# Gate matrices from two fp32r products, weighed twice by ACT, with a ring of three groups of one-hots

## The reference, cut to what matters

```python
q = (xb @ w_q).reshape(P_BLOCK, P_HEADS, 2, P_DKEY // 2)
s = einsum('thcd,hckd->thck', q, keys)
s_top, i_top = lax.top_k(s, 16)
cand = s_top[:, :, 0, :, None] + s_top[:, :, 1, None, :]
cand_idx = i_top[:, :, 0, :, None] * 128 + i_top[:, :, 1, None, :]
best, pos = lax.top_k(cand.reshape(..., 256), 16)
experts = take_along_axis(cand_idx.reshape(..., 256), pos)
gate = softmax(best)                       # 8 heads x 16 experts per token
act = gelu(einsum('thkd,td->thk', u_tab[experts], xb))
out = einsum('thk,thkd->td', gate * act, v_tab[experts])
```

## Time and profile before

| what | value |
|---|---|
| time, median of 3 runs | 5639.94 us (5639.61 to 5642.14) |
| the profiled execution's own time | 5643.49 us |
| its span, first to last instruction | 5641.7 us |
| mean granted PE clock | 0.907 of full speed |
| PE matmul busy | 4789.9 us (85%) |
| DVE busy | 2920.5 us (52%) |
| ACT busy | 1496.9 us (27%) |
| POOL busy | 1332.2 us (24%) |
| gate matmuls, L1912 | 2048 records, 249.9 us busy |
| weighing, L1812 | 1024 instructions, 312.5 us busy |
| one-hots, L1644 | 256 instructions, 381.8 us busy |

### The profile page before, as it was taken

How to read it: one execution, slowest core, us unless ns; L and a number is a source line. 1 busy time by engine, 2 the same in 40 slices (tenths; PEclk the granted TensorE clock), 3 DMA queues, 4 the chain that set the end, 5 groups by cost and what they waited for, 6 DMA issues and landing times. The chain is left out here.

```text
span 5641.7 us, 58879 instructions
## 1 busy us (share of the span) xinstructions
PE 4789.9 (85%) x22999; PEld 3849.3 (68%) x22999; DVE 2920.5 (52%) x4345; ACT 1496.9 (27%) x2767; POOL 1332.2 (24%) x571
## 2 busy tenths in 40 slices
PE   7885536667899999899998896666799999899998
PEld 2664316656688887788886364655688887788886
DVE  0124455431498884266664103751588883366665
ACT  1000100000145565222222001310255474222222
POOL 0000000000144444344443000000144443344442
PEclk9995558878999999999999897778999999999999
DMA  5210100002356686555554422002466686555552
GB/s 196 75 38 0 37 15 1 1 31 82 102 161 170 178 227 189 168 190 190 197 197 151 171 70 60 1 34 82 120 163 163 172 241 180 173 190 199 194 189 95
DMA packets 491349, 718.29 MB, mean 127 GB/s; under 512 B 46745, under 2 KB 341266, under 8 KB 468530
## 3 DMA queue, kind: packets, MB, share of 16 engines
q1 hardware_dynamic: 486466, 697.76, 39.5%
q0 software_dynamic: 4608, 16.78, 0.9%
HBM read 556.81 MB, written 153.40 MB: 126 GB/s over the span
## 5 line engine op out<-in xcount | busy, mean ns | idle before, releaser
L1880 PE MATMUL ps<-h_parts,u_parts 128*128 128x512 f32 x6144 | 1432.0, 393 | 62.5 <-POOL u_parts L1847 53.2
L2104 PE MATMUL ps<-w_parts,v_parts 128*128 128x512 f32 x6144 | 1397.5, 390 | 36.4 <-DVE w_parts L2089 36.4
L1880 PEld LDWEIGHTS ps<-h_parts,u_parts 128*128 128x128 f32 x6144 | 1152.0, 189 | 300.6 <-POOL u_parts L1847 53.8
L2104 PEld LDWEIGHTS ps<-w_parts,v_parts 128*128 128x128 f32 x6144 | 1156.2, 188 | 277.7 <-POOL v_parts L2075 37.2
L1847 POOL TENSOR_TENSOR u_parts<-u_turned,u_parts 128x1024 fp32r<-128x1024 f32 x256 | 658.2, 2571 | 2281.6 <-ACT u_parts L1800 2281.4
L2089 DVE TENSOR_TENSOR w_parts<-w_rows,w_parts 128x512 fp32r<-128x512 f32 x256 | 625.7, 2444 | 480.3 <-ACT w_parts L2068 480.3
L2075 POOL TENSOR_TENSOR v_parts<-v_rows,v_parts 128x1024 fp32r<-128x1024 f32 x256 | 615.2, 2403 | 817.8 <-ACT v_parts L2066 817.8
L194 PE MATMUL ps<-h,arena 128*128 128x264 f32 (+2 forms) x2176 | 488.7, 388 | 97.8 <-DMA arena<-in_even_w_out_dram 33.9
L194 PEld LDWEIGHTS ps<-h,arena 128*128 128x128 f32 (+1 forms) x2176 | 413.4, 190 | 174.4 <-DMA arena<-in_even_w_out_dram 34.3
L2066 ACT CAST v_parts<-v_rows 128x1024 fp32r<-128x1024 f32 x256 | 268.9, 1050 | 988.5 <-PE ps L2104 962.7
L1793 DVE STREAM_TRANSPOSE u_turned<-u_rows 128x1024 f32<-128x1024 f32 x256 | 317.1, 1239 | 301.3 <-POOL u_parts L1847 261.5
(11 more groups left out here) (457 smaller groups left out, 3920.3 us busy)
## 6 DMA issues: line engine op xcount, KB each, us to landing
u_rows<-in_peer_u_dram SPq DMA_DIRECT2D x1024, 128.0 KB, 3.6
v_rows<-in_peer_v_dram SPq DMA_DIRECT2D x128, 1024.0 KB, 4.9
hidden_tiles<-hidden SPq DMA_DIRECT2D x256, 256.0 KB, 3.5
gate_matrices<-h SPq DMA_DIRECT2D x64, 1024.0 KB, 7.2
gates<-gate_matrices SPq DMA_DIRECT2D x32, 2048.0 KB, 7.9
hidden_in<-hidden_tiles SPq DMA_DIRECT2D x256, 256.0 KB, 3.8
arena<-in_ada_w_dram SPq DMA_DIRECT2D x24, 2048.0 KB, 8.0
w_ring<-in_peer_w_q_dram SPq DMA_DIRECT2D x8, 2048.0 KB, 11.3
```

The lines of the kernel that those rows point to most:

```text
L1880: ins = mm(ps[:, n % 2, :], q.uTs[:, n % 3, wp, k, :], q.hs[:, xp, k, :], start=k == 0 and (wp, xp) == (0, 0), stop=k == DT - 1 and wp == 1)
L2104: ins = nc.tensor.matmul(ps[:, o, :], q.vs[:, n % 3, vp, o * P:(o + 1) * P], q.ws[:, n % 3, wp], start=n == 0 and (vp, wp) == (0, 0), stop ...
```

## The change

The shares are split into two fp32r numbers at each `settle`, a high part and the rest, held in `s.rs2`, a buffer that otherwise only the head norms of the mixers use. The one-hots buffer gets four parts per quad instead of two (row one-hot, column one-hot, row one-hot times the rest, row one-hot times the high part), in fp32r, and three slots instead of six, so its size stays. ACT makes both products. PE multiplies both with the column one-hot, as two fp32r matmuls that add up in PSUM.

```diff
-GATE_RING = 6
+GATE_RING = 3
...
             dve.wait_ge(q.chosen.sem, q.chosen.at(t + 1))
+            now_t = slice(t * P, (t + 1) * P)
+            link(v.tensor_copy(q.share[:, 0, now_t], q.choice[:, 2, now_t]))
+            link(v.tensor_tensor(q.share[:, 1, now_t], q.choice[:, 2, now_t], f32(q.share[:, 0, now_t]), ALU.subtract))
...
-                v.tensor_tensor(q.hot[:, k % GATE_RING], s.iota[:].unsqueeze(1).unsqueeze(1).to_broadcast(eight),
+                hot = q.hot[:, k % GATE_RING]
+                v.tensor_tensor(hot[:, 0:2], s.iota[:].unsqueeze(1).unsqueeze(1).to_broadcast(eight),
...
         for i in range(4):
-            row = q.hot[:, k % GATE_RING, 0, i, :]
-            ins = nc.scalar.mul(row, row, q.choice[:, 2, 4 * k + i:4 * k + i + 1])
+            hot, at = q.hot[:, k % GATE_RING, :, i, :], slice(4 * k + i, 4 * k + i + 1)
+            nc.scalar.mul(hot[:, 2], f32(hot[:, 0]), f32(q.share[:, 1, at]))
+            ins = nc.scalar.mul(hot[:, 3], f32(hot[:, 0]), f32(q.share[:, 0, at]))
...
                         for i in range(4):
-                            ins = mm(ps[:, 2 + k % 4, i * P:(i + 1) * P], q.hot[:, k % GATE_RING, 0, i, :],
-                                     q.hot[:, k % GATE_RING, 1, i, :], start=True, stop=True)
+                            for part in (3, 2):
+                                ins = mm(ps[:, 2 + k % 4, i * P:(i + 1) * P], q.hot[:, k % GATE_RING, part, i, :],
+                                         q.hot[:, k % GATE_RING, 1, i, :], start=part == 3, stop=part == 2)
...
-            q.hot = whole("onehots", [P, GATE_RING, 2, 4, P])
+            q.hot = s.sb(f"onehots{layer}", [P, GATE_RING, 4, 4, P], second, F32R)
+            q.share = s.rs2[:, :, 0:T].bitcast(F32R)
```

## The result

The changed kernel takes 5944.0 us (median of 4 runs, 5937.1 to 5953.5), the one before 5641.0 beside it: ratio 1.0533 [1.0511, 1.0554], 303 us slower. The forecast was 5815 in a range of 5750 to 5900. The direction was right, the size was not: 303 us in place of 175.

A forecast was written before the change was run, and what follows sets the result against it. PE bounds the kernel before, ACT the gate stretches after. A 27.7, B 27.7, C 30 and the rest 2 make 87.4 us a layer, 175 in all: 5818 on the profiled execution, 5815 as median, range 5750 to 5900.

The forecast's parts named there:

- A: First stretch making gate matrices in layer 0 (1660 to 1746 us): 17.3 us from slower units plus 10.4 store waits, 27.7.
- B: Second stretch making gate matrices in layer 0 (1820 to 1906 us): the same growth as A, 27.7 us.
- C: Third stretch making gate matrices in layer 0 (1985 to 2217 us), 64 quads in 26 units: growth of 30 us.
- ACT becomes the bound, 9.87 us a unit: Three-quad units: twelve more multiplications at 0.293 us raise ACT from 6.36 to 9.87 us, above PE's 8.14.
- The fp32r record at 0.109 us: PE's gate products: a 128-column fp32r record taken like the f32 one, 0.108 us, 0.87 us a quad, no gain or loss.
- the rival of slow fp32r records: Gate products on PE: fp32r records at 0.233 us add 253 us in place of the main case, 5893; chance 0.22.
- So the ring adds no wait of its own beyond the first unit: One-hots in a ring of three: gates and one-hots are ready before ACT wants them, so no term for the ring.
- The lead: Ring of three: it takes away the lead with which ACT could have started; no price of its own.
- Store waits, exposed and 5.2 us each: ACT's gate copies waiting for gate stores, hidden under PE before: two each in A and B, 10.4 us per stretch.
- The rival that they shrink: Gate-store waits: slower units give stores more room, 48 us less, 5767; chance 0.12.
- the 0.9 that I had named as a sign against me: PE's granted clock in A and B: a value under 0.9 would show the prediction wrong.
- The clock rival: An idler PE drops to the 1.2 GHz level: 6200 in some 60 units, 5940 for a third of it; chance 0.06.

The follow-up runs named there:

- doubling alone: Kernel before, ring of six and f32 products kept, with four more ACT multiplications (by ones) per quad: 5833.4 us, ratio 1.0324.
- ring alone: Kernel before with only the ring of one-hots cut from six to three quads: 5768.4 us, ratio 1.0228.
- e5: Kernel before with a single fp32r product per token (rest of the share left out), ring of six: 5602.1 us, ratio 0.9926.
- e10: Kernel before with a ring of three, and SP issuing older gate stores ahead of the hidden stores: 5713.5 us, ratio 1.0130.
- e11: Changed kernel with six unused 512-column matmuls (the filler) on PE in A and B units of three or more quads: 5943.7 us, ratio 1.0523.

## Why the prediction was wrong, step by step

Growth of the three stretches in us (first gates to start of the last), forecast against runs:

| stretch | forecast | doubling alone | ring alone | the change |
|---|---|---|---|---|
| A | 27.7 | 27.3 | 17.4 | 42.0 |
| B | 27.7 | 27.7 | 17.6 | 44.6 |
| C | 30 | 28.4 | 24.4 | 54.8 |

- **ACT becomes the bound, 9.87 us a unit: right.** Multiplications stand 0.29 us apart, also with fp32r outputs, and undisturbed units take 9.6 to 9.9. The Trainium skill (ScalarE: Activation LUTs, What ACT_TABLE_LOAD costs) gives an ACTIVATE with one pointer operand 280 ns + 0.833 ns a column, of which some 93 ns overlap with the next. The estimate from it for 128 columns is 294 ns apart, and the trace agrees with 0.293 us. The forecast's terms for A, B and C hit the doubling alone within 2 us each. In A that is partly luck: up to the last hidden product it takes 104.1 us there, forecast 104.5, but 3.0 less before the second hidden product, 4.5 more in the two store waits, and 1.8 less in the others.
- **The fp32r record at 0.109 us: right.** 24 of them take 2.63 us (1660.75 to 1663.38 in the rows above), 12 take 1.29 in e5. So the rival of slow fp32r records is out. The Trainium skill (TensorE: Matmul & The Clock Gate, Back-to-back issue gap) has about 81 ns each for a stream of 128-column products. Here the trace does not agree: neither form goes under 0.108 us.
- **"So the ring adds no wait of its own beyond the first unit": wrong, and this is the step that failed.** The ring costs 127 us alone. I followed undisturbed units of three quads, where it holds (9.9 us), and laid the quads of each unit side by side. I put this term at nothing. But a ring of three is closed over DVE, ACT and PE: the one-hot of quad k waits for the gates of k-3, these for a PSUM bank, that for ACT's copy of k-7, and ACT copies only in its next iteration, behind the weighing of every quad before it. In a four-quad unit the fourth one-hot (1669.93) waits for the only gates that PE has been able to make, ACT weighs it until 1673.5, then copies, and PE goes on at 1674.73; the next one-hots wait for those gates, and ACT idles 3.55 us. Two things lengthen this last link. The first 8 gate records behind the wait take 0.22 us each, some 0.9 us more than at 0.108. And the one-hot that starts at 1676.71, 1.23 us by itself, is still out when POOL's subtraction ends at 1678.93; ACT goes on at 1680.04. Each link was in my working, but not closed to a loop: the interval from the first to the second hidden product comes to 12.5 us there (9.3 + 2.8 + 3.0, less the 2.6 of the first gates), and takes 16.5.
- **The lead,** that is, how far ACT's weighing is ahead of PE. The prediction saw that the ring "takes away the lead with which ACT could have started" and gave that no price. The lead is what covers a store wait: with six slots ACT has weighed ahead, with three PE stops. By itself the ring exposes these waits; e10 puts them at 55 of its 127 us, with the limit named there.
- **Store waits, exposed and 5.2 us each: exposed, but too small.** In A the two idle 6.73 and 5.16 us, and their units take 8.5 and 6.9 more than 9.87, so 15.4 in place of 10.4. That is the doubling's doing and not the ring's: with six slots and the doubled ACT the same units take 8.3 and 6.6 more. The order of stores is worth 64 us on the changed kernel. The rival that they shrink is out.
- **A put together:** 116.8 us from first gates to last hidden, where the forecast had 104.5. Of the 12.3 missing, 4.0 fall before the second hidden product, 5.0 in the store waits, and 3.3 in the other six intervals (12.3, 10.2 and 10.7 in place of 9.87 just behind the four-quad unit, the last three undisturbed). Against the doubling alone A takes 12.7 us more: 7.1 before the second hidden product, 3.9 in the next three intervals, 1.3 behind the first store wait, and 0.5 in the store waits themselves. So what the ring adds to the change in A is above all the loop of the four-quad unit.
- **C, 30 us: too small by 25.** Its start was right in kind: PE's idle time grows from 6.36 to 12.82 us, the forecast's 6.5. But from the first gates to those behind that wait C takes 2131.47 - 2074.72 = 56.8 us, before 2028.04 - 1988.37 = 39.7: 17.1 more, since a four-quad unit lies in it (15.9 us, before 9.1), with a slower one behind it (10.4, before 8.1). That is 10.6 of the 25 missing; the other 14 lie behind it, where PE waits again and again for ACT's copies, 3.43 us at the longest. PE in C of the changed kernel, first gates, those behind the long wait, and a late unit, beside the earlier trace rows:

```profile
2074.72 1.48 PE L1918 MATMUL ps<-onehots 128*128 128x128 f32 x8 [2.33 <-ACT onehots L1817]
...
2131.47 1.97 PE L1918 MATMUL ps<-onehots 128*128 128x128 f32 x8 [12.82 <-ACT onehots L1817]
...
2307.21 3.48 PE L1918 MATMUL ps<-onehots 128*128 128x128 f32 x16 [3.43 <-ACT h L1825]
```

- **The clock: no large part, but not shown to be off the path.** It did fall to 0.82 and 0.80, under the 0.9 that I had named as a sign against me. The clock rival's number for a third of the units, 5940, lies 4 us from the measured time; that is chance and no support, for its PE would be busy all the time, and here PE is idle 23 of 126 us in A. e11 raised the mean clock without a gain, with the limits named there. Where ACT waits 1.21 us for a one-hot behind gates at 0.22 us a record, the slow gates (3.65 us in place of 1.97) could be the reason; that is argued and not shown.
- **Chances.** The case that came was on no list: the forecast's mechanism with a second one beside it. The range ended 44 us short, because its upper end was made of one rival and not of the mechanism's own unknowns.

Open: how the 72 us that e10 leaves of the ring divide between four-quad units, one-hots held by POOL, and C.

## What to carry to other kernels

Before shrinking a ring, follow the whole loop that it closes, other rings and in-order queues included, for the fullest and the most delayed step and not for the average one; a ring that is shorter than the largest batch of one step needs a price of its own. Lead between engines is what hides waits of fixed length: where a change takes the lead, every wait hidden today has to be added, and with what comes behind it. When an engine becomes too slow for uneven portions, try to even them out first: one number gave back 263 of 303 us here.

## What the runs showed of the hardware

- A PE record of 128 columns takes 0.108 to 0.110 us, for half an f32 product and for a whole fp32r product alike, while one of 512 columns takes 0.233. So in this kernel fp32r halves a 128-column f32 product, and two fp32r products are worth nothing against one f32. What sets the 0.108 wasn't tried.
- After an idle PE of 4.6 to 4.8 us in stretch A of the changed kernel, gate records take 0.22 us each (24 in 5.36 us, granted clock 0.50 from 1674.80 to 1680.00, the 1.2 GHz level), and the run of 24 hidden products behind them 6.9 to 7.6 us in place of 5.7. The filler did not change that (24 gate records in 5.35 us, hidden 7.0 to 7.9), though it raised the mean clock of the window.
- A one-hot on DVE takes 1.23 us by itself. Three take 3.50 us in the earlier trace rows, and 5.57 us where a subtraction of POOL (2.36 us) is under way as they start.
